# Attention stage: the projection round split 5/8 and 3/8 around the transposes, and the next unit's scores on other steps

## The reference, cut to what matters

```
xn = rms_norm(x, norm_g)
qa, ka, va, za, qb, kb, vb, zb = split(xn @ w_in)
# 4 heads "diff": two 64-wide queries and keys per head, values 128 wide
qa, ka = rms_norm per head
s1 = q1 @ k1.T * scale + t5_bias;  s2 = q2 @ k2.T * scale + t5_bias
oa = (softmax(s1) - lam * softmax(s2)) @ v
ya = rms_norm(oa) * (1 - lam_init) * silu(za)
# 8 heads "neighbourhood": 64 wide, keys within an 8 x 16 window of a 16 x 64 grid
yb = softmax(q @ k.T * scale + rpb, masked) @ v * silu(zb)
x = x + concat(ya, yb) @ w_out
```

## Time and profile before

| | us |
|---|---|
| median of 3 runs | 3287.28 |
| lowest, highest | 3286.69, 3287.87 |
| profiled execution | 3286.93 |
| its span in the trace | 3285.1 |
| units 0 to 6 of the attention stage | 98.2 to 754.4 |

### The profile page before, as it was taken

The page is one execution under the profiler, slowest core; times in us unless marked ns, Lnnn a source line. Parts: engine busy times, 40 slices in busy tenths (PEclk is TensorE's granted clock), DMA queues, the critical chain, the costliest instruction groups (busy, mean ns, idle before and its releaser), DMA issues.

```text
span 3285.1 us, 48721 instructions
## 1 busy us (share of the span) xinstructions
PE 3125.3 (95%) x17764; PEld 2652.4 (81%) x17764; DVE 2021.6 (62%) x3766; ACT 1059.9 (32%) x2057; POOL 1428.3 (43%) x1207
## 2 busy tenths in 40 slices
PE   8988888888998899999999999999999999999998
PEld 7776676677898788988888888888889888888886
DVE  4656555565588721377777775655553687777776
ACT  3444444353113311142222221454442422222221
POOL 6533424332654333475555554421103665555534
PEclk9999999999999999999999999999999999999999
DMA  6211111105211211201111111000001111111111
GB/s 193 64 51 38 51 38 38 50 14 193 87 62 33 56 55 41 91 26 52 51 51 51 51 51 68 26 14 17 17 14 65 39 65 51 51 51 51 51 53 62
DMA packets 181817, 179.39 MB, mean 55 GB/s; under 512 B 50235, under 2 KB 163067, under 8 KB 181499
## 3 DMA queue, kind: packets, MB, share of 16 engines
q1 hardware_dynamic: 181566, 177.02, 17.0%
q10 hardware_dynamic: 96, 0.26, 0.0%
HBM read 160.12 MB, written 22.38 MB: 56 GB/s over the span
## 4 chain that ended last, share of the span: by engine, by line
PE 61%; DVE 2%; ACT 1%; issue 1%; POOL 0%; POOLq 0%; DVEq 0%; ACTq 0%
PE banks L2749 16%; PE banks L79 13%; PE banks L81 13%; PE banks L80 13%; PE banks L3566 2%; PE banks L3543 1%; PE banks L215 1%; PE banks L3500 0%; PE banks L3501 0%; PE banks L3482 0%; POOL x L183 0%; PE banks L3509 0%; PE banks L2371 0%; POOL rstd L178 0%; DVE stats L168 0%
## 5 line engine op out<-in xcount | busy, mean ns | idle before, releaser
L2986 DVE TENSOR_TENSOR x<-x,banks 128x512 f32<-128x512 f32 x784 | 523.3, 687 | 240.1 <-PE banks L2749 231.7
L79 PE MATMUL banks<-winhi,xt_hi 128*128 128x512 f32 (+1 forms) x576 | 225.7, 392 | 11.7 <-ACT vz L978 5.7
L80 PE MATMUL banks<-winlo,xt_hi 128*128 128x512 f32 (+1 forms) x576 | 216.3, 376 | 0.0
L81 PE MATMUL banks<-winhi,xt_lo 128*128 128x512 f32 (+1 forms) x576 | 215.6, 374 | 0.0
L79 PE MATMUL banks<-h1t_hi,f1w_buf_hi 128*128 128x512 f32 x512 | 199.5, 390 | 1.6 <-issue 1.6
L79 PE MATMUL banks<-h3t_hi,f2w_buf_hi 128*128 128x512 f32 x512 | 199.5, 390 | 1.6 <-issue 1.6
L81 PE MATMUL banks<-h3t_hi,f2w_buf_lo 128*128 128x512 f32 x512 | 199.2, 389 | 0.0
L81 PE MATMUL banks<-h1t_hi,f1w_buf_lo 128*128 128x512 f32 x512 | 199.2, 389 | 0.0
L80 PE MATMUL banks<-h1t_lo,f1w_buf_hi 128*128 128x512 f32 x512 | 199.2, 389 | 0.0
L80 PE MATMUL banks<-h3t_lo,f2w_buf_hi 128*128 128x512 f32 x512 | 199.2, 389 | 0.0
L1001 ACT ACTIVATE scores<-scores,mixsmall 128x1024 f32<-128x1024 f32 (+2 forms) x128 | 122.5, 957 | 186.7 <-DVE mixsmall L1171 186.5
(11 more groups left out here) (549 smaller groups left out, 9389.3 us busy)
## 6 DMA issues: line engine op xcount, KB each, us to landing
f1w_raw<-in_w_ff SPq DMA_DIRECT2D x32, 1024.0 KB, 5.2
f2w_raw<-in_w_ff SPq DMA_DIRECT2D x32, 1024.0 KB, 5.2
winraw<-in_w_in SPq DMA_DIRECT2D x128, 128.0 KB, 2.5
gluw_raw<-in_ssm_w_glu SPq DMA_DIRECT2D x14, 512.0 KB, 4.5
x<-in_x SPq DMA_DIRECT2D x8, 512.0 KB, 6.4
wow_raw<-in_w_out SPq DMA_DIRECT2D x4, 1024.0 KB, 5.8
x<-in_x SPq DMA_DIRECT2D x1, 4096.0 KB, 15.5
gew_raw<-in_w_ple_gate SPq DMA_DIRECT2D x4, 1024.0 KB, 5.2
```

The lines of the kernel that those rows point to most:

```text
L79: nc.tensor.matmul(out, a.hi, b.hi, start=start, stop=False)
L80: nc.tensor.matmul(out, a.hi, b.lo, start=False, stop=False)
L81: return nc.tensor.matmul(out, a.lo, b.hi, start=False, stop=stop)
L2986: nc.vector.tensor_tensor(xx, xx, chip.ps[:, 4 + 2 * (p % 2) + g, :], ALU.add).then_inc(s_acc, 1)
```

## The change

TensorE, units 0 to 6: the round is cut into `project(..., range(0, 5))` and `project(..., range(5, 8))`. Between them stand output transposes (steps 1 and 4) and head transposes (steps 5 and 6), in both kinds of unit; the values come after the second part. The next unit's first scores are issued at the end of step 6, the second ones in step 7 after the first part of the round. Unit 7 keeps its order. Head and output transposes get waits on the copies out of banks 4 and 5 (`s_ta`, `s_td`).

ScalarE: `out_hi` of D units and `head_hi` stand after the exponentials, then `squares`, `out_hi` of N units, and `taken` last. Before the sigmoid stands a wait on its own reads of bank 6. VectorE: `biased(g + 2)` stands ahead of `combine` or `scale_rows`, `head_scale` ahead of `gated` and `out_lo`, and `variance` last. The orders of GpSimd and SyncE are as before.

```
@@ TensorE @@
+                        project(PROLOGUE + g, range(0, FIRST))
                         if t == 7:
-                            scores(g + 1)
-                        project(PROLOGUE + g)
+                            scores(g + 2)
...
-                    if t == 1 and u and UNITS[u - 1][0] == "N":
+                    if t == 1 and u and (more or UNITS[u - 1][0] == "N"):
                         out_transposes(u - 1, 1)
-                    if t == 4 and UNITS[u][0] == "N":
-                        out_transposes(u, 0)
-                    values(g)
...
+                    if t == 4 and (more or UNITS[u][0] == "N"):
                         out_transposes(u, 0)
                     if more and t == 5:
                         head_transposes(u + 1, (0, 1))
                     if more and t == 6:
                         pe.wait_ge(s_ql, 4 * (u + 1) + 2)
                         head_transposes(u + 1, (2, 3))
-                    if more and t == 7:
+                    if more:
+                        project(PROLOGUE + g, range(FIRST, KT))
+                    values(g)
...
+                    if more and t == 6:
                         scores(g + 2)
@@ VectorE @@
+                    if t < 6 and more:
+                        biased(g + 2)
                     if kind_of(g + 1) == "D":
                         combine(g + 1)
                     elif kind_of(g + 1) == "N":
                         scale_rows(g + 1)
-                    if t < 6 and more:
-                        biased(g + 2)
@@ ScalarE @@
                     if t == 0:
                         act.wait_ge(s_gate, 2 * u)
+                        act.wait_ge(s_pe, TAKEN[PROLOGUE + NT * u])
...
+                    if more and t in (5, 6):
+                        head_hi(u + 1, 2 * (t - 5))
+                        head_hi(u + 1, 2 * (t - 5) + 1)
+                    if more or t < 7:
+                        squares(g)
...
+                    if more:
+                        taken(PROLOGUE + g)
+                        if t == 7:
                             expo(g + 2, 0)
                             down(g + 2)
                             expo(g + 2, 1)
```

More of the change, by code:

```diff
@@ L746, in distance_bias, with project @@
                                  start=True, stop=True).then_inc(s_cm, 1)
-            def project(r):
+            def project(r, ks=range(KT)):
                 cs, j = ROUNDS[r]
@@ L758, in project @@
                     out, rows = chip.ps[:, 6, 0:CH], lambda cs, k: chunk_rows(cs[0], k)
-                for k in range(KT):
+                for k in ks:
                     last = mm3(nc, out, m.xt.at(slice(None), k, slice(j * P, j * P + P)), rows(cs, k), k == 0, k == KT - 1)
-                last.then_inc(s_p, 1)
+                if ks[-1] == KT - 1:
+                    last.then_inc(s_p, 1)
             def head_transposes(u, groups):
                 pe.wait_ge(s_qn, NT * (u + 1))
+                if u:
+                    pe.wait_ge(s_ta, NT * (u - 1) + 6 + groups[0] // 2)
+                    pe.wait_ge(s_td, NT * (u - 1) + 6 + groups[0] // 2)
                 for a in groups:
@@ L937, in _ @@
                         head_transposes(u + 1, (2, 3))
-                    if more and t == 7:
+                    if more:
+                        project(PROLOGUE + g, range(FIRST, KT))
+                    values(g)
+                    if not more and t == 1 and UNITS[u - 1][0] == "D":
+                        out_transposes(u - 1, 1)
+                    if not more and t == 4 and UNITS[u][0] == "D":
+                        out_transposes(u, 0)
+                    if more and t == 6:
                         scores(g + 2)
@@ L1319, in _ @@
                             gated(u - 1, 1)
-                        else:
-                            out_lo(u - 1, 1)
+                        out_lo(u - 1, 1)
                     if t == 4:
-                        if dense:
-                            out_lo(u, 0)
-                        else:
+                        if not dense:
                             gated(u, 0)
-                    if a < NT * NU:
-                        head_scale(a)
-                    if dense:
-                        variance(g)
-                    if t == 1 and u and dense:
-                        out_lo(u - 1, 1)
-                    if t == 4 and not dense:
                         out_lo(u, 0)
@@ L1339, in _ @@
                         biased(g + 2)
+                    if dense:
+                        variance(g)
             finish(STEPS - 1)
```

56 lines of the change are left out of this document (25 added, 31 removed).

## The result

The changed kernel takes 3187.32 us (median of four executions, 3183.66 to 3189.08), the kernel before, on the same chip, 3286.99. The ratio is 0.970, with an interval from 0.968 to 0.971. The profiled execution took 3183.66 us; that of before took 3286.93. The difference between the profiles is 103.3 us, and it has two parts.

What follows compares the result with a forecast made beforehand. TensorE, busy 95% of the span, was taken as the bound, standing 85 us in units 0 to 6 in seven small chains. Idle 69 plus clock 16 made 85 us saved: 3287 - 85 = 3202 us, range 3184 to 3240.

Steps and rivals of the forecast that it cites:

- Head transposes: Probability transposes' 14 waits on the head parts, 39.0 us: hidden except about 1.4 in unit 6, saving 37.6 us.
- Low parts of the output: Four waits after dense units, 11.5 us: covered except about 2.0 in unit 6, saving 9.5 us.
- Grid steps' copy: Twelve waits for VectorE's copy of the last head rows, 17.3 us: 7.3 left including 0.48 floors, saving 10.0 us.
- Scores: Next unit's score matmuls waiting for the bias to empty banks 0 to 3, 9.0 us: spread out, saving 7.7 us.
- Bank 6: Rounds waiting for ScalarE to empty bank 6, 4.1 us: about 2.6 left, in dense step 6, saving 1.5 us.
- VectorE's slack: VectorE's 8.0 us chain from variance to head scale ends 1.4 us before the next probability transposes are due.
- the clock: Units 0 to 6: TensorE's time lost at 1.2 GHz mostly returns as long waits go, saving 16 us, bounds 0 and 27.
- Bank 6 as the bound: Dense steps: late squares and reads make bank 6 the wait, about 38 us, giving 3240 us; chance 0.13.
- The port between VectorE and GpSimd: Dense steps 4 and 5: combination waits for GpSimd's mask addition under a shared lock, 7 us, giving 3209; chance 0.10.
- Slower through the combination: Dense steps: combination, now last, delays probability transposes, costing from 1.4 us over; 3317 us at 5 over; chance 0.03.
- No effect: Last unit and the product behind it are set by transfers, so the gain is returned there, 3287 us; chance 0.03.
- All covers and the clock: Units 0 to 6: every cover holds and the clock stays up, giving 3184 us; chance 0.06.

Runs made afterwards that it cites:

- the two runs with copies: Changed kernel with VectorE's copy of bank 5 in each dense step made one more time, or four more times: 3183.34 us and 3215.35 us.
- the two with fillers: Kernel before with unused matmuls ahead of probability transposes: 3388.6 us with 28 to 80 of them, 3267.52 us with 7, 12 or 18.

## Why the prediction was right, and where it was off

The forecast was 3202, in a range from 3184 to 3240; the result is 3187.3. The direction, the two-part structure and nearly every wait came as worked out.

- **Head transposes**: 39.0 to 1.4 forecast, to 1.5 measured, in unit 6 as said.
- **Low parts of the output**: 11.5 to 2.0 forecast, to 1.9 measured, in unit 6.
- **Grid steps' copy**: 17.3 to 7.3 forecast, to 6.0 measured. The floor of 0.48 us stands in nine waits, and step 5 has 0.55 and not 1.0.
- **Grid output product**: 3.8 to 0.9 forecast, to nothing.
- **Scores**: 9.0 to 1.3, as forecast; the run with the scores as before confirms 6.6 of it.
- **Bank 6**: 4.1 to 2.6 forecast, to 1.4 in three waits of 0.5 in dense step 6, the place that was named; the 0.8 us in front of unit 7 was not foreseen.
- **VectorE's slack** of 1.4 us: between 0.7 and 2.9 by the two runs with copies.
- **Idle time**: 69.2 us saved forecast, 72 measured.

**The step that was off is the clock.** The prediction bounded the loss at 33 us, took two thirds of it as falling on busy time, 22, and left 6 of that in place: 16 us saved. By the clock record the bound was 31, and 28 of it fell on busy time: nine tenths, not two thirds. Of these 1.5 remained, at unit 0's start, not 6. The busy time measured 26.8 us less, the whole of the stated best case of 27. The place was too narrow as well: the prediction saw the drop behind the wait of 5.64 us, but 9 of the 13 drops lie at waits under 3 us, and shortening the long waits alone gave no clock back (the run with bias first). With 26.8 in place of 16, and 72 in place of 69, the sum is 99, and the median fell by 99.7. "Units 0 to 6 take about 571 us" was too high for the same reason; they take 557.

**The rivals.** Bank 6 as the bound (0.13): wrong, 1.4 us. The port between VectorE and GpSimd (0.10): the mechanism is there, and L1204, which ends with GpSimd's mask addition to within 0.02 us six times, shows it, in agreement with the exclusive lock of the Trainium skill, "SBUF — State Buffer", "Who interferes with whom"; but its price was nothing, since the low parts ended 0.26 us inside the cover. Slower through the combination (0.03): the point from which it costs is bracketed by the runs with copies; its price of 32 steps was too high, since at 2.9 us over it would be 48 us, and 28 was measured, 10 of it clock. No effect (0.03): the last unit moved with the rounds, as argued. All covers and the clock (0.06, 3184): this is the nearest to what happened, and it had too small a chance.

What the prediction did not say is how the parts depend on each other. TensorE's order alone gave 14 us, the bias alone 22, against the kernel before on the same chip; in the changed kernel, taking away ScalarE's order costs 53, the cut 18, the bias 16 and the scores 5. The cover in TensorE's list has no effect as long as the reader of the banks stands behind something that comes after the cover.

## What to carry to other kernels

When work is moved so as to hide a chain between engines, follow the whole chain: each engine on it must also have it ahead of anything that waits for the covering work. A distribution of many small waits by releaser, priced against cover one by one, gives a sound sum. Price the clock separately: in these runs it came back with the number of waits of about 2 us or more that were gone, and not in proportion to the idle time. Making a long wait shorter but leaving it at 2 us gave no clock back.

## What was not expected of the hardware

The clock goes with the number of long waits, not with the idle time. With 85, 75, 64 or 48 us of idle time in the seven units, 23 to 27 us of TensorE's time were lost to the lower level (1.2 GHz) all the same. These four kernels have 17 to 24 waits of 1.9 us or more and 12 to 15 drops. With 5 waits and 4 drops the loss was 10.5 us, with 4 and 3 it was 5.9, with one of each 2.9, and without a drop nothing. That is 1.6 to 2.9 us for each drop.

Where the drops lie is the same everywhere. In the thirteen kernels (the two with fillers included) there are 66 drops in units 0 to 6 behind unit 0's start, and every one begins during a wait of 1.9 us or more or within 1.6 us after its end. There are 99 such waits, so about two in three have one. No wait of 1.8 us or less has one, and the kernel with the scores as before has over twenty of 0.5 to 1.6. The length of a wait alone does not tell whether it has one. In the kernel before, two waits of the same length, 2.00 us (ended at 249.31) and 1.99 us (ended at 262.96), have these stretches behind them, the first at a clock of 0.50 and the second at 1.00:

```profile
250.90:254.20 3.30, 3.30 (x12) 2.17 (x9) 3.23 (x8) 0.36 (x2) 1.52 (x2) 0.50 0.00 0
263.20:266.60 3.40, 3.40 (x20) 2.92 (x19) 2.53 (x5) 0.60 (x1) 3.11 (x3) 1.00 0.01 2
```

What decides between them is open.

A float32 matmul of 128x128 cost 0.225 us in a row of eighty (18.03 us), while in the trace each of its records is 0.27 to 0.28 us long and they overlap.
